# Depthwise convolution taps of the sample tokens: from VectorE to GpSimd, one tap of all four chunks with each step of the page loads

## Chip, cores and metric

The kernel runs on one core of a Trainium2 chip. The metric is the time of one execution on the device in microseconds (us), here the median of three runs. TensorE's clock has two levels, 1.2 and 2.4 GHz; the profile gives the granted clock as a share of the full one.

## What is computed

One layer of a decoder with two groups of tokens, 1024 of a prompt and 64 of samples (8 sequences of 8 new tokens). Every token passes three branches (a convolution module, sparse attention over selected keys, attention over a memory), which are merged and followed by a feed-forward part. Two pieces matter here. They don't depend on each other.

```python
# convolution: 31 taps per channel (512 channels), for prompt and sample tokens
c = conv(u_ext, w_dw)                 # c[t, ch] = sum_k u_ext[t + k, ch] * w_dw[k, ch]
c = silu(layernorm(c + b_dw, g_ln, b_ln))
# indexer scores of the sample tokens over 4096 cached keys each, which lie in pages of 128
ki_past = cache_idx_k[page_table]
I = sum_h w[t, h] * relu(q_idx[t, h] . ki[s] / 8)
```

For the sample tokens `u_ext` is 30 cached rows and 8 new ones of each sequence.

## The kernel before, in words

The program is a row of stages. Each is a block with a program of its own for every engine; at its end all engines meet at a barrier (`end_phase`, L2619 to L2624), and semaphores are cleared. `build` (L2610) calls the stages in order; the one that matters is `stage_sample_score` (L2018), between the first and the second half of the input products.

In this stage two things go on side by side.

The first is the scoring of the cached keys, in 32 steps (`NSTEP`). A step takes 8 pages, four for each of two sequences. Four of them go into one half of a slot and four into the other; there are four slots (`NSL`). The loads are shared out: SP issues three pages of the first sequence, GpSimd three of the second, ScalarE the fourth of both (`load_page`, L2035). A load reads the page's number into a register (L2039) and issues a DMA (L2040). From step 4 on, the issuing engine first waits until TensorE has turned the pages of four steps ago (`s_turn`). TensorE transposes the four pairs of pages of a step (`turn`, L2061, products on L2067), ScalarE copies the result out of PSUM (L2122), TensorE forms the dot products (`dots`, L2075), ScalarE applies relu (L2128), and TensorE adds up the heads (`wsum`, L2083). At the end come four small pairs of products for the new keys (L2098, L2101) with a relu between them (L2138).

The second is the convolution, on VectorE (L2141 to L2161). Channels lie on the partitions in four chunks (`KC`), tokens along the free dimension. For each of 31 taps (`CW`) and each chunk there are two instructions, one for the 1024 prompt tokens and one for the 64 sample tokens, each of which multiplies by the tap's weight of the channel and adds to what stands in `cT`. Tap 0 starts from the bias instead (L2152), the others are fused (L2155). A tap of a chunk waits for the tap before of the same chunk, four pairs earlier (L2147). When all taps are done, VectorE waits for the last weighted sum of TensorE and adds a mask to it (L2159), which is the last operation of the stage.

The order of the work on an engine is the order in which the program is written; nothing reorders it. GpSimd has nothing in this stage but its 96 loads:

```python
            def load_pages(eng, par):
                for n in range(NSTEP):
                    if n >= NSL:
                        eng.wait_ge(s_turn, n - NSL + 1)
                    for g in range(PPC - 1):
                        load_page(eng, page_in[par], n, g, par)
```

The prediction also reads rows of other stages, for what GpSimd and VectorE take there: the sample part of the gated input on GpSimd (L1153), the last scaling of the layer norm on VectorE (L1657), the split of the merge weights on GpSimd (L2281) beside a sum on VectorE (L2252), the split of the merged activations on both (L2322), a scaled difference on VectorE (L2495), and the indirect loads of keys by GpSimd (L689).

Of the kernel before, what the change touches and what calls it, by code (L numbers as in the profile page):

```python
# [11 lines left out]
F32 = mybir.dt.float32  # L12
# [3 lines left out]
ALU = mybir.AluOpType  # L16
# [3 lines left out]
P = 128  # L20
# [3 lines left out]
SEQ = 1024  # L24
NSEQ, TDEC = 8, 8
NS = NSEQ * TDEC
NT = SEQ + NS
# [4 lines left out]
DC, CW = 512, 31  # L32
KC = DC // P
# [37 lines left out]
PPC = 4  # L71
# [1946 lines left out]
def stage_sample_score(nc, m, score):  # L2018

    NQ = 2 * NPAIR  # L2020
    NSTEP = NC2 * NQ
    with ExitStack() as ctx:
        NSL = 4
# [4 lines left out]
        page_in = [[m.sem(f"ik_page_in_{e}{i}") for i in range(NSL)] for e in ("sync", "gpsimd", "scalar")]  # L2028

        s_turn, s_kev = m.sem("ik_page_turned"), m.sem("ik_T_ready")  # L2030
        s_dots, s_relu, s_ws = m.sem("ik_dots"), m.sem("ik_relu_s"), m.sem("ik_wsum")
        s_hev = [m.sem(f"ik_half_evac{i}") for i in range(2)]
        s_end, tap = m.sem("ik_end"), m.sem("conv_taps")
        with nc.Block() as block:
            def load_page(eng, arrived, n, g, par):  # L2035
                r, q = n // NQ, n % NQ
                hf, i = q // NPAIR, q % NPAIR
                at = r * PPC + (2 * i + par) * NPAGE + hf * NC2 * PPC + g
                phys = eng.value_load(m.pages[0:1, at:at + 1], min_val=0, max_val=NPHYS - 1)  # L2039
                eng.dma_start(page[:, n % NSL, g, par, :].rearrange("p (a d) -> p a d", a=1),  # L2040
                              m.cache_idx_k[bass.ds(phys, 1)].rearrange("a p d -> p a d")).then_inc(arrived[n % NSL], 16)

            def load_pages(eng, par):

                for n in range(NSTEP):
                    if n >= NSL:
                        eng.wait_ge(s_turn, n - NSL + 1)
                    for g in range(PPC - 1):
                        load_page(eng, page_in[par], n, g, par)

            @block.sync
            def _(sp):
                load_pages(sp, 0)

            @block.gpsimd
            def _(pool):
                load_pages(pool, 1)

            @block.tensor
            def _(pe):  # L2060
# [80 lines left out]
            @block.vector  # L2141
            def _(dve):
                nc.vector.memset(score[0:64, HALF:SW], NEG).then_inc(s_end, 1)
                for k in range(CW):
                    for c in range(KC):
                        if k >= 1:
                            dve.wait_ge(tap, 2 * ((k - 1) * KC + c + 1))  # L2147
                        for dst, src in ((m.cT[:, c, 0:SEQ], m.u[:, c, k:k + SEQ]),
                                         (m.cT[:, c, SEQ:NT].rearrange("p (s t) -> p s t", s=NSEQ),
                                          m.us[:, c, :, k:k + TDEC])):  # L2150
                            if k == 0:
                                nc.vector.tensor_scalar(dst, src, m.wdw[:, c, 0:1], m.bdw_sb[:, c:c + 1],  # L2152
                                                        ALU.mult, ALU.add).then_inc(tap, 1)
                            else:
                                nc.vector.scalar_tensor_tensor(out=dst, in0=src, scalar=m.wdw[:, c, k:k + 1], in1=dst,  # L2155
                                                               op0=ALU.mult, op1=ALU.add).then_inc(tap, 1)
                dve.wait_ge(tap, 2 * CW * KC)
                dve.wait_ge(s_ws, NSTEP + NPAIR)
                nc.vector.tensor_tensor(score[64:128, HALF:SW], m.B[5][64:128, 0:NS], m.newmask[64:128, :], ALU.add  # L2159
                                        ).then_inc(s_end, 1)  # L2160
                dve.wait_ge(s_end, 2)  # L2161
# [448 lines left out]
def build(nc, io):  # L2610
    with ExitStack() as ctx:
# [62 lines left out]
        stage_first_products(nc, m)  # L2674
        end_phase()
        stage_sample_score(nc, m, m.sscore)
        end_phase()
        c_ki.close()
# [75 lines left out]
```

## Time and profile before

| | |
|---|---|
| median of 3 runs | 2603.65 us (2603.33 to 2607.54) |
| profiled execution: its time, its span | 2609.0 us, 2607.4 us |
| busy over the span | TensorE 86%, VectorE 51%, GpSimd 31%, ScalarE 23% |
| mean granted TensorE clock | 0.928 |
| the stage | from 540.6 us, closing add at 711.6 us, next stage from 713.2 us |

Times in the rows are us from the start of the span unless marked ns. PE is TensorE, PEld its weight loads, DVE VectorE, ACT ScalarE, POOL GpSimd. A timeline row has the start, the duration, the engine, the line, the operation, what it writes and reads, the shape and the count, and in brackets the idle time before it with what ended it. A group of instructions has busy time and mean ns of one, and then the idle time before them. Neighbouring instructions of an engine overlap by some hundredths of a us, so what one costs is the distance of starts. "issue" is time in which an engine waited for nothing that the profile shows.

### The profile page before, as it was taken

The numbers are of one execution on the slowest core, as the hardware profiler recorded it, in microseconds if no ns is written. First come the engines' busy times: TensorE is split into PE (matmuls) and PEld (weight loads), VectorE is DVE, ScalarE is ACT, GpSimd is POOL, SyncE is SP. The second block draws the span as 40 slices with busy tenths as digits, with TensorE's granted clock in tenths as the row PEclk, the third lists the DMA queues.
The fourth block names the chain that finished last, engine by engine and source line by source line (L and its number), as shares of the span: only waits on it lengthen the run. The fifth ranks groups of instructions, "written<-read, shape, count | busy, mean of one in ns | idle before, by whom it ended". The sixth has DMA issues, their size and how long they took to land. (4 is left out here: it accounts for less than half of the span.)

```text
span 2607.4 us, 37427 instructions
## 1 busy us (share of the span) xinstructions
PE 2229.6 (86%) x14085; PEld 2044.7 (78%) x14102; DVE 1338.9 (51%) x2216; ACT 596.2 (23%) x1066; POOL 801.2 (31%) x591
## 2 busy tenths in 40 slices
PE   5959988967289998666667879699999999999997
PEld 5829988932079998555445679698999999999997
DVE  5089998079959992395677454433111111111123
ACT  4152212223031211132233331222210111111112
POOL 4102211134011221257667412434222231222231
PEclk9988998989599999886688999899999999999999
DMA  5001112223032221467877434411111111111112
GB/s 178 21 17 50 47 45 89 84 72 75 1 126 90 92 66 41 163 212 265 279 222 229 136 129 139 157 48 40 41 40 53 44 36 53 41 46 43 49 32 93
DMA packets 229221, 240.04 MB, mean 92 GB/s; under 512 B 37011, under 2 KB 192704, under 8 KB 226669
## 3 DMA queue, kind: packets, MB, share of 16 engines
q1 hardware_dynamic: 183723, 124.76, 16.2%
q0 software_dynamic: 23552, 70.28, 8.6%
q10 hardware_dynamic: 21834, 43.55, 4.5%
q8 instruction: 66, 1.08, 0.2%
q14 instruction: 46, 0.38, 0.0%
HBM read 207.91 MB, written 30.98 MB: 92 GB/s over the span
## 5 line engine op out<-in xcount | busy, mean ns | idle before, releaser
L387 PE MATMUL banks<-ffn_in_hi,ffn_w_hi 128*128 128x384 f32 (+1 forms) x1032 | 339.1, 329 | 5.3 <-POOL ffn_w_lo L402 3.8
L388 PE MATMUL banks<-ffn_in_lo,ffn_w_hi 128*128 128x384 f32 (+1 forms) x1032 | 338.8, 328 | 0.0
L389 PE MATMUL banks<-ffn_in_hi,ffn_w_lo 128*128 128x384 f32 (+1 forms) x1032 | 338.8, 328 | 0.0
L402 POOL TENSOR_TENSOR ffn_w_lo<-ffn_w_raw,ffn_w_hi 128x1024 fp32r<-128x1024 f32 (+2 forms) x84 | 180.4, 2148 | 409.1 <-ACT ffn_w_hi L201 409.1
L387 PE MATMUL banks<-halves,ffn_w_hi 128*128 128x384 f32 (+1 forms) x654 | 214.4, 328 | 22.7 <-PEq L2324 22.7
L389 PE MATMUL banks<-halves,ffn_w_lo 128*128 128x384 f32 (+1 forms) x654 | 214.3, 328 | 0.0
L388 PE MATMUL banks<-halves,ffn_w_hi 128*128 128x384 f32 (+1 forms) x654 | 214.2, 328 | 0.0
L387 PEld LDWEIGHTS banks<-ffn_in_hi,ffn_w_hi 128*128 128x128 f32 x1032 | 195.1, 189 | 6.1 <-issue 4.0
L387 PE MATMUL banks<-h_hi,second_w_hi 128*128 128x384 f32 (+1 forms) x576 | 190.6, 331 | 7.3 <-POOL second_w_lo L235 5.6
L388 PEld LDWEIGHTS banks<-ffn_in_lo,ffn_w_hi 128*128 128x128 f32 x1032 | 195.0, 189 | 0.0
L389 PEld LDWEIGHTS banks<-ffn_in_hi,ffn_w_lo 128*128 128x128 f32 x1032 | 195.0, 189 | 0.0
L389 PE MATMUL banks<-h_hi,second_w_lo 128*128 128x384 f32 (+1 forms) x576 | 189.9, 330 | 0.0
L388 PE MATMUL banks<-h_lo,second_w_hi 128*128 128x384 f32 (+1 forms) x576 | 189.9, 330 | 0.0
L689 POOL DMA_INDIRECT k_rows_got<-in_cache_k,sel_row x128 | 137.6, 1075 | 144.3 <-POOLq L2623 62.4
L2155 DVE SCALAR_TENSOR_TENSOR room<-room,w_dw 128x1024 f32<-128x1024 f32 x240 | 167.1, 778 | 0.0
L1305 DVE TENSOR_SCALAR_CACHE_REDUCE mask<-room,sel_cand 128x384 bf16<-128x384 f32 (+1 forms) x186 | 163.7, 942 | 1.1
L387 PE MATMUL banks<-h_hi,first_w_hi 128*128 128x384 f32 (+1 forms) x480 | 160.2, 334 | 4.3 <-POOL first_w_lo L402 4.3
L388 PE MATMUL banks<-h_lo,first_w_hi 128*128 128x384 f32 (+1 forms) x480 | 159.7, 333 | 0.0
L389 PE MATMUL banks<-h_hi,first_w_lo 128*128 128x384 f32 (+1 forms) x480 | 159.7, 333 | 0.0
L2295 DVE TENSOR_TENSOR x<-banks,x 128x384 f32 (+1 forms) x96 | 50.9, 536 | 205.4 <-PE banks L389 183.3
L699 POOL DMA_INDIRECT v_rows_got<-in_cache_v,sel_row x128 | 129.3, 1010 | 67.5 <-issue 37.5
L201 ACT CAST ffn_w_hi<-ffn_w_raw 128x1024 fp32r<-128x1024 f32 (+2 forms) x84 | 79.2, 944 | 307.4 <-PE banks L389 281.2
(377 smaller groups left out, 4847.5 us busy)
## 6 DMA issues: line engine op xcount, KB each, us to landing
ffn_w_raw<-in_w_ffn_in SPq DMA_DIRECT2D x44, 512.0 KB, 3.7
merge_gate<-gate_spill_dram SPq DMA_DIRECT2D x24, 544.0 KB, 3.9
first_w_raw<-in_w_in SPq DMA_DIRECT2D x24, 512.0 KB, 3.8
second_w_raw<-in_w_in SPq DMA_DIRECT2D x24, 512.0 KB, 3.8
ffn_w_raw<-in_w_ffn_out SPq DMA_DIRECT2D x24, 384.0 KB, 3.3
gate_spill_dram<-second_out ACTq DMA_DIRECT2D x16, 544.0 KB, 2.7
room<-q_spill_dram ACTq DMA_DIRECT2D x8, 1024.0 KB, 6.9
q_spread<-q_spill_dram ACTq DMA_DIRECT2D x8, 1024.0 KB, 6.6
```

The lines of the kernel that those rows point to most:

```text
L201: self.m.nc.scalar.copy(self.w_hi[:, s, 0:g.kc, :], self.raw[:, s, 0:g.kc, :]).then_inc(self.hi_done, 1)
L387: nc.tensor.matmul(out, self.w_hi[:, s, k, :], g.hi[:, k, a:a + w], start=(k == 0), stop=False)
L388: nc.tensor.matmul(out, self.w_hi[:, s, k, :], g.lo[:, k, a:a + w], start=False, stop=False)
L389: mm = nc.tensor.matmul(out, self.w_lo[:, s, k, :], g.hi[:, k, a:a + w], start=False, stop=(k == g.kc - 1))
L402: self.m.nc.gpsimd.tensor_tensor(self.w_lo[:, s, 0:g.kc, :], self.raw[:, s, 0:g.kc, :], self.w_hi[:, s, 0:g.kc, :], ALU.subtract).then_inc ...
L689: pool.indirect_dma_start(self.keys[:, n % self.K_SLOTS, f, :], None, rows, bass.IndirectOffsetOnAxis(ap=m.sel_row[:, f, n:n + 1], axis=0) ...
L699: pool.indirect_dma_start(self.values[:, v % self.V_SLOTS, f, :], None, rows, bass.IndirectOffsetOnAxis(ap=m.sel_row[:, f, v:v + 1], axis= ...
L1305: c = nc.vector.tensor_scalar(m.mask[:, MOFF[b]:MOFF[b + 1]], sl(b), lim, 0.0, op, ALU.add, accum_out=cnt[:, j:j + 1])
L2155: nc.vector.scalar_tensor_tensor(out=dst, in0=src, scalar=m.wdw[:, c, k:k + 1], in1=dst, op0=ALU.mult, op1=ALU.add).then_inc(tap, 1)
L2295: nc.vector.tensor_tensor(x, m.B[3 * s + n][:, 0:w].rearrange("p (a n) -> p a n", a=1), x, ALU.add).then_inc(gemm.emptied[s], 1)
```

## The change

VectorE keeps the prompt part of each tap only. GpSimd takes the sample part: after the three loads of step n (n below 31) it does tap n for all four chunks at once, as a product of 4 x 8 x 8 columns with a broadcast weight into a new buffer, and an add of that product to `cT` (for tap 0: of the product to the broadcast bias). The add waits for the product, the product for the add of the tap before. VectorE's counts of its own semaphore are halved, and at the end it waits for all 62 operations of GpSimd as well. SP's loads stay as they are.

```diff
-                for n in range(NSTEP):
-                    if n >= NSL:
-                        eng.wait_ge(s_turn, n - NSL + 1)
-                    for g in range(PPC - 1):
-                        load_page(eng, page_in[par], n, g, par)
+            def load_pages_of(eng, par, n):
+                if n >= NSL:
+                    eng.wait_ge(s_turn, n - NSL + 1)
+                for g in range(PPC - 1):
+                    load_page(eng, page_in[par], n, g, par)
...
             def _(pool):
-                load_pages(pool, 1)
+                made = ctx.enter_context(nc.sbuf_tensor("conv_sample_product", [P, KC, NS], F32))
+                made4 = made[:, :, :].rearrange("p c (s t) -> p c s t", s=NSEQ)
+                out = m.cT[:, :, SEQ:NT].rearrange("p c (s t) -> p c s t", s=NSEQ)
+
+                def sample_tap(k):
+                    w = m.wdw[:, :, k].unsqueeze(2).unsqueeze(3).to_broadcast([P, KC, NSEQ, TDEC])
+                    if k >= 1:
+                        pool.wait_ge(stap, 2 * k)
+                    nc.gpsimd.tensor_tensor(made4, m.us[:, :, :, k:k + TDEC], w, ALU.mult).then_inc(stap, 1)
+                    pool.wait_ge(stap, 2 * k + 1)
+                    b = m.bdw_sb[:, :].unsqueeze(2).unsqueeze(3).to_broadcast([P, KC, NSEQ, TDEC])
+                    nc.gpsimd.tensor_tensor(out, made4, out if k else b, ALU.add).then_inc(stap, 1)
+
+                for n in range(NSTEP):
+                    load_pages_of(pool, 1, n)
+                    if n < CW:
+                        sample_tap(n)
...
                         if k >= 1:
-                            dve.wait_ge(tap, 2 * ((k - 1) * KC + c + 1))
-                        for dst, src in ((m.cT[:, c, 0:SEQ], m.u[:, c, k:k + SEQ]),
-                                         (m.cT[:, c, SEQ:NT].rearrange("p (s t) -> p s t", s=NSEQ),
-                                          m.us[:, c, :, k:k + TDEC])):
...
+                            dve.wait_ge(tap, (k - 1) * KC + c + 1)
+                        dst, src = m.cT[:, c, 0:SEQ], m.u[:, c, k:k + SEQ]
...
-                dve.wait_ge(tap, 2 * CW * KC)
+                dve.wait_ge(tap, CW * KC)
+                dve.wait_ge(stap, 2 * CW)
                 dve.wait_ge(s_ws, NSTEP + NPAIR)
```

## Rows read from the trace of the kernel before

**Rows 1.** Timeline of VectorE, in short windows of the stage.

```profile
540.64 3.92 DVE L2152 TENSOR_SCALAR room<-room,w_dw,params 128x1024 f32<-128x1024 f32 x8
544.48 1.27 DVE L2155 SCALAR_TENSOR_TENSOR room<-room,w_dw 128x1024 f32<-128x1024 f32 x1
...
545.67 0.27 DVE L2155 SCALAR_TENSOR_TENSOR room<-room,w_dw 128x64 f32<-128x64 f32 x1
...
545.87 1.27 DVE L2155 SCALAR_TENSOR_TENSOR room<-room,w_dw 128x1024 f32<-128x1024 f32 x1
...
547.07 0.27 DVE L2155 SCALAR_TENSOR_TENSOR room<-room,w_dw 128x64 f32<-128x64 f32 x1
...
711.60 0.23 DVE L2159 TENSOR_TENSOR room<-banks,newmask 64x64 f32<-64x64 f32 x1
```

**Rows 2.** Groups of instructions, shapes apart, from 530 to 760 us.

```profile
L2155 DVE SCALAR_TENSOR_TENSOR room<-room,w_dw 128x1024 f32<-128x1024 f32 x120 | 153.4, 1278 | 0.0
L2155 DVE SCALAR_TENSOR_TENSOR room<-room,w_dw 128x64 f32<-128x64 f32 x120 | 33.4, 278 | 0.0
...
L1657 DVE SCALAR_TENSOR_TENSOR room<-room,params,second_out 128x1088 f32<-128x1088 f32 x1 | 1.4, 1350 | 1.2 <-ACT second_out L1594 1.2
...
L2040 POOL DMA_DIRECT2D ik_page<-in_cache_idx_k x96 | 51.6, 537 | 85.0 <-issue 79.6 <-PE banks L2067 5.5
```

**Rows 3.** Stretches: length; busy PE, PEld, DVE, ACT, POOL; PE clock, DMA, GB/s.

```profile
600.00:653.00 53.00, 38.17 (x123) 13.40 (x122) 53.00 (x78) 20.06 (x35) 24.46 (x46) 1.00 0.31 74
653.00:665.00 12.00, 8.68 (x31) 3.69 (x30) 12.00 (x18) 3.63 (x9) 0.12 (x1) 0.96 0.01 3
665.00:711.00 46.00, 0.00 (x0) 0.00 (x0) 46.00 (x67) 0.00 (x0) 0.00 (x0) 0.50 0.00 0
724.00:729.00 5.00, 0.00 (x0) 0.00 (x0) 4.96 (x12) 2.10 (x3) 2.38 (x2) 0.98 0.59 148
729.00:733.00 4.00, 3.98 (x14) 3.98 (x15) 0.00 (x0) 2.10 (x2) 2.31 (x1) 0.59 0.60 148
```

**Rows 4.** Timeline of GpSimd: third and fourth page load, and the last.

```profile
544.42 0.53 POOL L2040 DMA_DIRECT2D ik_page<-in_cache_idx_k  x1 [0.57 <-issue]
545.57 0.53 POOL L2040 DMA_DIRECT2D ik_page<-in_cache_idx_k  x1 [0.62 <-issue]
...
652.59 0.53 POOL L2040 DMA_DIRECT2D ik_page<-in_cache_idx_k  x1 [0.61 <-issue]
```

**Rows 5.** Timeline of TensorE: its last products of the stage.

```profile
664.41 0.48 PE L2101 MATMUL banks<-ik_relu,w_sel 128*64 128x64 f32 x2 [0.31 <-ACT ik_relu L2138]
```

**Rows 6.** Lines L1153 and L2281: duration min/median/max in ns, first and last start.

```profile
L1153 POOL TENSOR_TENSOR u_new<-glu_pair x4: 320/322/325, 237.4 to 309.4; 128x64 f32<-128x64 f32 x4
...
L2281 POOL TENSOR_TENSOR merge_w_lo<-merge_w_raw,merge_w_hi x24: 1262/1569/2210, 1520.5 to 1660.5; 128x512 fp32r<-128x512 f32 x24
```

**Rows 7.** Timelines of GpSimd and VectorE where the merged activations are split.

```profile
1674.40 2.48 POOL L2322 TENSOR_TENSOR halves<-room,halves 128x1088 fp32r<-128x1088 f32 x1 [12.64 <-ACT halves L2336]
...
1676.84 3.53 POOL L2322 TENSOR_TENSOR halves<-room,halves 128x1088 fp32r<-128x1088 f32 x1
...
1675.36 2.68 DVE L2322 TENSOR_TENSOR halves<-room,halves 128x1088 fp32r<-128x1088 f32 x1 [2.56 <-ACT halves L2336]
...
1677.96 3.57 DVE L2322 TENSOR_TENSOR halves<-room,halves 128x1088 fp32r<-128x1088 f32 x1
...
1681.45 3.57 DVE L2322 TENSOR_TENSOR halves<-room,halves 128x1088 fp32r<-128x1088 f32 x1
```

**Rows 8.** Timelines of GpSimd and VectorE in the merge.

```profile
1558.87 2.21 POOL L2281 TENSOR_TENSOR merge_w_lo<-merge_w_raw,merge_w_hi 128x512 fp32r<-128x512 f32 x1 [4.66 <-ACT merge_w_hi L2261]
...
1558.65 1.29 DVE L2252 TENSOR_TENSOR room<-room,merge_gate 128x1088 f32<-128x1088 f32 x1
```

**Rows 9.** Line L2495: duration min/median/max in ns, first and last start.

```profile
L2495 DVE SCALAR_TENSOR_TENSOR ffn_in_lo<-x,params,ffn_in_hi x8: 2425/2428/2429, 1710.2 to 1793.2; 128x1088 fp32r<-128x1088 f32 x8
```

**Rows 10.** Timeline of GpSimd: an indirect load right behind another.

```profile
1082.64 0.96 POOL L689 DMA_INDIRECT k_rows_got<-in_cache_k,sel_row  x1 [0.30 <-issue]
```

More of the change, by code:

```diff
@@ L2032, in stage_sample_score @@
         s_hev = [m.sem(f"ik_half_evac{i}") for i in range(2)]
-        s_end, tap = m.sem("ik_end"), m.sem("conv_taps")
+        s_end, tap, stap = m.sem("ik_end"), m.sem("conv_taps"), m.sem("conv_sample_taps")
         with nc.Block() as block:
@@ L2041, in load_page @@
                               m.cache_idx_k[bass.ds(phys, 1)].rearrange("a p d -> p a d")).then_inc(arrived[n % NSL], 16)
-            def load_pages(eng, par):
-                for n in range(NSTEP):
-                    if n >= NSL:
-                        eng.wait_ge(s_turn, n - NSL + 1)
-                    for g in range(PPC - 1):
-                        load_page(eng, page_in[par], n, g, par)
+            def load_pages_of(eng, par, n):
[3 more added lines that the diff above has]
+                    load_page(eng, page_in[par], n, g, par)
             @block.sync
             def _(sp):
-                load_pages(sp, 0)
+                for n in range(NSTEP):
+                    load_pages_of(sp, 0, n)
             @block.gpsimd
             def _(pool):
-                load_pages(pool, 1)
+                made = ctx.enter_context(nc.sbuf_tensor("conv_sample_product", [P, KC, NS], F32))
[9 more added lines that the diff above has]
+                    nc.gpsimd.tensor_tensor(out, made4, out if k else b, ALU.add).then_inc(stap, 1)
+                for n in range(NSTEP):
+                    load_pages_of(pool, 1, n)
+                    if n < CW:
+                        sample_tap(n)
             @block.tensor
@@ L2146, in _ @@
                         if k >= 1:
-                            dve.wait_ge(tap, 2 * ((k - 1) * KC + c + 1))
-                        for dst, src in ((m.cT[:, c, 0:SEQ], m.u[:, c, k:k + SEQ]),
-                                         (m.cT[:, c, SEQ:NT].rearrange("p (s t) -> p s t", s=NSEQ),
-                                          m.us[:, c, :, k:k + TDEC])):
[L2151 to L2156, printed above, removed]
-                dve.wait_ge(tap, 2 * CW * KC)
+                            dve.wait_ge(tap, (k - 1) * KC + c + 1)
+                        dst, src = m.cT[:, c, 0:SEQ], m.u[:, c, k:k + SEQ]
+                        if k == 0:
+                            nc.vector.tensor_scalar(dst, src, m.wdw[:, c, 0:1], m.bdw_sb[:, c:c + 1],
+                                                    ALU.mult, ALU.add).then_inc(tap, 1)
+                        else:
+                            nc.vector.scalar_tensor_tensor(out=dst, in0=src, scalar=m.wdw[:, c, k:k + 1], in1=dst,
+                                                           op0=ALU.mult, op1=ALU.add).then_inc(tap, 1)
+                dve.wait_ge(tap, CW * KC)
+                dve.wait_ge(stap, 2 * CW)
                 dve.wait_ge(s_ws, NSTEP + NPAIR)
```

## Prediction

> **What bounds the kernel now.** I read the stage that the diff touches and nothing else, because a barrier stands before it and behind it: whatever its end moves by, the run moves by. The first view is the timeline of VectorE. The convolution starts at 540.64 us and runs without a gap until the closing add (L2159) at 711.60 [rows 1]. The groups by shape say of what: 120 taps of 128x1024 and 120 of 128x64 [rows 2]. The reader is to see the starts, not the durations, since neighbours overlap: the small tap at 545.67 is followed by a large one at 545.87 and by the next small one at 547.07 [rows 1]. So a small tap holds VectorE for 0.20 us (its duration says 0.27) and a large one for 1.20, which makes 1.39 for a pair, and 120 such pairs from 544.48 on (167 us) are the rest of the stretch.
>
> The second view is busy time by stretch. TensorE and ScalarE are done by 665: from 665 to 711 VectorE alone works, TensorE at 1.2 GHz (granted 0.50) doing nothing [rows 3]. So the pages have 46 us of slack, and the question is how much of it the change eats.
>
> The third is the timeline of GpSimd. It issues 96 page loads, three to a step, one start every 1.14 to 1.15 us (544.42, 545.57), each 0.53 of work on the engine and 0.61 of issue, the last at 652.59 [rows 2, 4]. TensorE ends 12.3 us after that last issue, at 664.41 + 0.48 = 664.89 [rows 5]. GpSimd's program order therefore paces the pages at 3 x 1.145 = 3.43 us a step, and what is put between its loads delays the pages directly. Its waits on turned pages come to 5.5 us in all [rows 2].
>
> **The change part by part.**
>
> *Removed from VectorE:* 4 + 120 small taps. 124 x 0.196 = 24.3 us (0.20 unrounded). Alone, the convolution would end at 711.6 - 24.3 = 687.3. The four taps k = 0 lose four small ones too, so the first fused tap starts at 543.7 instead of 544.48. The halved semaphore counts cost nothing: a tap still waits for the one four instructions earlier.
>
> *Added to GpSimd:* 31 products and 31 adds of 128x256. The same operation took 0.322 us for 64 columns and, undisturbed, 1.262 for 512 [rows 6]: 2.10 ns a column, so 0.725 us for 256. The broadcast weight and the 4x8x8 patterns are not in the trace; I take no surcharge, with 0 and +0.3 us as bounds. 62 x 0.725 = 45 us of bare work, by itself inside the slack of 46.
>
> *Both engines at once.* This decides. Where VectorE and GpSimd run operations with two SBUF inputs side by side, they take turns [rows 7]: GpSimd's first operation, begun before VectorE's, took 2.48 us, its next one 3.53, and VectorE's went to 2.68 and 3.57, while an operation of that size alone takes VectorE 1.29 [rows 8]. In the steady part both have a pitch of 3.49 (1677.96 to 1681.45), which is one VectorE turn (about 1.21) plus one GpSimd turn (2.28). [rows 8] show the same from one side: the VectorE operation ends at 1559.94, GpSimd's 512 columns at 1561.08, 1.14 later, against 1.262 alone. So a GpSimd turn is its duration less 0.12 to 0.20: 0.53 to 0.60 for 256 columns, and I take 0.58. VectorE's operation ends 1.16 after GpSimd's (1680.37 to 1681.53 in [rows 7]); for 1024 columns instead of 1088, 1.08. The convolution's own instruction is of this kind: the fused form with two SBUF inputs took 2.43 us at all eight places where GpSimd was subtracting beside it [rows 9], and 1.35 elsewhere [rows 2].
>
> The opposite reading deserves its price. The Trainium skill, "Advanced Engine Details and Errata", section VectorE Performance Modes, warns of blocking between GpSimd and Vector instructions in a two-port mode, and names no others. The fused tap is in no faster mode (1.20 us for 1024 columns, 1.17 ns each), so by that note alone nothing would be blocked and the time would be that of the first rival, 2597; by the turns of [rows 7] it is 2627. The trace disagrees with the note as far as it goes, since [rows 7, 9] slow down all the same.
>
> *VectorE with turns:* 687.3 + 62 x 0.58 = 723.3. That is already 12 us behind today's end.
>
> *GpSimd with turns.* Let an add end at time 0. VectorE's waiting tap ends at 1.08, the next at 2.28, the next at 3.47. GpSimd issues three loads, starts 1.145 apart, the third finished 2.82 after the first starts; the first starts 0 to 0.6 after the add. (The row nearest is the gap between back-to-back indirect issues, 0.30 [rows 10], and I take that; 0.6 is the idle time before a page load [rows 4].) The product thus asks at 2.8 to 3.4, before 3.47, and gets its turn there: over at 4.05. The add waits for the product by semaphore, so VectorE gets the turn between (5.13), and the add ends at 5.71. So a tap and its step take **5.71 us** instead of 3.43, and VectorE does four taps in it, which is the one k that those four chunks make: both queues finish nearly together.
>
> The first product asks at 544.95, when the third load is done [rows 4]. VectorE's tap just then ends at 544.95 too, so I count the next (546.15); the other choice is worth 1.2 us. The add of k = 0 then ends at 548.4, that of k = 30 at 548.4 + 30 x 5.71 = 719.7. Behind it on GpSimd's queue stand the loads of step 31: the last starts at 719.7 + 0.3 + 2.29 = 722.3, and 12.3 us of tail follow, as today. The closing add starts at 734.6 instead of 711.6: **+23.0 us**.
>
> *The new waits.* VectorE's wait for all sample taps is over at 719.7, long before its wait for the last weighted sum: nothing. The product's wait for the former add is over too. The add's wait for the product is in the sum (it gives VectorE its turn between). What queues behind on GpSimd is the three loads of the next step, for which TensorE waits, then ScalarE's copies and its own two loads (behind the copies in its queue), then VectorE at the very end. The loads on SP go further ahead and wait for turned pages: nothing.
>
> *TensorE's clock.* In today's page loop it stands at 2.4 GHz with 38.2 us busy in 53 [rows 3]. The same work would spread over 5.71 us a step. From 724 to 729 TensorE did nothing, and the products after it ran at a granted 0.59 [rows 3]. Should the level fall in the page loop too, the tail with its 8.7 busy us [rows 3] would grow, by 0 to about 6 us; I take 0, the level that the page loop has today, and keep the 6. After the stage, the memory's second products start behind a weight transfer issued after the barrier, which shifts with it: 0, with up to 1.5 us to win if the clock is higher there.
>
> The profiled execution took 2609.0 us (span 2607.4), the median is 2603.65. Both stages are the same work, so I put the +23 on the median: 2626.65, **2627**.
>
> **The rivals.**
>
> *No turns for these shapes* (not slower). VectorE ends at 687.3; The add, once sent off, runs under the preparation of the next load, so a step is three loads of 1.145, the 0.53 of the third that the product must wait for, 0.73 of product and some 0.07 of hand-over: 4.76. The add of k = 30 would end near 689.5, the last load start at 692, the stage end at 704.3, which is -7 us: 2597, and -3 if the add is not covered. It decides once a tap costs the page loop less than 46.7 / 31 = 1.5 us. The idle 0.61 before each load is for it; [rows 7, 9] are against it.
>
> *VectorE alone sets the end.* If GpSimd prepares loads while its add waits, the product could ask before 2.28; the step is then 4.52, the pages end near 699, and VectorE's 723.3 decides: +12, 2616. For it: preparation and work of two loads do overlap. Against: the loads' own 2.82.
>
> *A turn later.* If a load can start only 0.65 us or more after the add, or the product costs 0.3 more, the request misses the boundary at 3.47 and the step is 6.91 with five VectorE taps. After 24 such taps VectorE is done, the last six go at some 4.9: add k = 30 at 745, end at 760: +48, 2652.
>
> **How the numbers follow.** Forecast (2622 to 2634 with the clock's bound): 0.63. VectorE's end alone: 0.13. A turn later: 0.14. No turns: 0.08. Something past 2652: 0.02. The range takes in the two slower rivals and leaves out the last two: 2613 to 2652. A measurement of this kernel tells 0.2% (5.2 us) from no change. No turns lies on both sides of that, so faster 0.05, same 0.04, slower 0.91.
>
> **What would show it.** In the changed profile: large taps 1.20 apart where GpSimd loads, and about 1.78 (1.20 + 0.58) apart around a product or an add; products and adds of 0.7 us drawn out to 1.2 to 1.9; triples of page loads about 5.7 us apart instead of 3.43; the last load near 722; the closing add near 735, released by TensorE and no longer by VectorE's own taps. Taps 1.20 apart all the way would prove me wrong about the turns, a last load before 705 about what sets the end, and steps of 6.9 about the boundary.

## The result, and the profile after

The changed kernel takes 2614.96 us (median of seven executions, the lowest 2609.41) against 2603.65 before. The ratio is 1.0036 with an interval of 1.0023 to 1.0049, so it is 9.4 us (6.0 to 12.8) slower. One of the seven executions, and four of six in a later comparison, took 2738 to 2741 us; the ratios are of the others, and the second half of the experiments is about the long ones. The profiled execution took 2618.74 us, its span is 2617.1.

The difference lies in the one stage. The timeline of VectorE in the changed kernel, in short windows: the stage's first instruction, four neighbouring prompt taps, the closing add:

```profile
540.80 0.11 DVE L2158 MEMSET room<- 64x64 f32 x1 [93.28 <-PEq L2637]
...
568.22 1.27 DVE L2168 SCALAR_TENSOR_TENSOR room<-room,w_dw 128x1024 f32<-128x1024 f32 x1
...
569.41 1.92 DVE L2168 SCALAR_TENSOR_TENSOR room<-room,w_dw 128x1024 f32<-128x1024 f32 x1
...
571.25 1.74 DVE L2168 SCALAR_TENSOR_TENSOR room<-room,w_dw 128x1024 f32<-128x1024 f32 x1
...
572.92 1.27 DVE L2168 SCALAR_TENSOR_TENSOR room<-room,w_dw 128x1024 f32<-128x1024 f32 x1
...
721.88 0.23 DVE L2173 TENSOR_TENSOR room<-banks,newmask 64x64 f32<-64x64 f32 x1
```

From first instruction to closing add are 181.1 us, against 171.0 before [rows 1]; what follows takes 1895.2 after and 1895.8 before. Read the starts: an undisturbed tap still costs 1.20 (568.22 to 569.41), the next two 1.84 and 1.67. The small taps are gone, and the closing add has no idle time before it: VectorE's own taps still set the end.

GpSimd in the same stretch, one step of the pages, and its last load:

```profile
567.16 0.57 POOL L2040 DMA_DIRECT2D ik_page<-in_cache_idx_k  x1
567.90 0.53 POOL L2040 DMA_DIRECT2D ik_page<-in_cache_idx_k  x1 [0.17 <-issue]
569.04 0.53 POOL L2040 DMA_DIRECT2D ik_page<-in_cache_idx_k  x1 [0.61 <-issue]
569.60 0.64 POOL L2064 TENSOR_TENSOR conv_sample_product<-room,w_dw 128x256 f32<-128x256 f32 x1
570.32 1.60 POOL L2067 TENSOR_TENSOR room<-conv_sample_product,room 128x256 f32<-128x256 f32 x1
571.86 0.57 POOL L2040 DMA_DIRECT2D ik_page<-in_cache_idx_k  x1
...
692.69 0.53 POOL L2040 DMA_DIRECT2D ik_page<-in_cache_idx_k  x1 [0.61 <-issue]
```

A step is 571.86 - 567.16 = 4.70 us (3.43 before, [rows 4]; 5.71 predicted). Two things are to be seen. The first load of the next step starts at 571.86, when the add ends: it was prepared while the add still waited. And the product (569.60) takes 0.64 us, its bare time, although VectorE had begun a tap at 569.41; it is that tap that grows to 1.92. Only the add waits (1.60). So a step holds three taps of VectorE and what the two operations hold them up by: 3 x 1.20 + 0.64 + 0.47 = 4.71.

Two of the 31 products of this profile did wait, and theirs are the only steps above 5.1 us. One of them:

```profile
552.13 0.57 POOL L2040 DMA_DIRECT2D ik_page<-in_cache_idx_k  x1
552.88 0.53 POOL L2040 DMA_DIRECT2D ik_page<-in_cache_idx_k  x1 [0.17 <-issue]
554.34 0.53 POOL L2040 DMA_DIRECT2D ik_page<-in_cache_idx_k  x1 [0.93 <-issue]
554.89 1.25 POOL L2064 TENSOR_TENSOR conv_sample_product<-room,w_dw 128x256 f32<-128x256 f32 x1
556.22 1.58 POOL L2067 TENSOR_TENSOR room<-conv_sample_product,room 128x256 f32<-128x256 f32 x1
557.75 0.58 POOL L2040 DMA_DIRECT2D ik_page<-in_cache_idx_k  x1
```

Its third load came 0.32 us later than in other steps, the product asked 0.50 us into a tap, waited (1.25), and the step took 557.75 - 552.13 = 5.62 us with a fourth tap in it. The other late one asked at 0.48 us and took 1.29; the 29 that asked 0.17 to 0.47 us into a tap all took 0.63 to 0.65.

The groups of instructions of the changed kernel, shapes apart, from 530 to 780 us, answer to [rows 2]:

```profile
L2168 DVE SCALAR_TENSOR_TENSOR room<-room,w_dw 128x1024 f32<-128x1024 f32 x120 | 178.1, 1561 | 0.0
...
L2040 POOL DMA_DIRECT2D ik_page<-in_cache_idx_k x96 | 53.0, 552 | 51.8 <-issue 51.8
L2067 POOL TENSOR_TENSOR room<-conv_sample_product,room 128x256 f32<-128x256 f32 x30 | 48.0, 1599 | 2.4
L2064 POOL TENSOR_TENSOR conv_sample_product<-room,w_dw 128x256 f32<-128x256 f32 x31 | 21.0, 678 | 0.5
```

And the stretches (columns as in [rows 3]), with TensorE's last products of the stage from its timeline behind them:

```profile
600.00:653.00 53.00, 36.32 (x93) 12.06 (x94) 53.00 (x35) 14.06 (x24) 43.15 (x57) 0.81 0.24 57
...
705.00:721.00 16.00, 0.08 (x1) 0.00 (x0) 16.00 (x15) 0.00 (x0) 0.00 (x0) 0.50 0.00 0
```

```profile
704.61 0.47 PE L2116 MATMUL banks<-ik_relu,w_sel 128*64 128x64 f32 x2 [0.31 <-ACT ik_relu L2153]
```

The pages are done at 705.08, and 16 of the 46 us of slack are left. TensorE's granted clock in the page loop went from 1.00 to 0.81, but its tail from the last load on is 12.4 us against 12.3 before [rows 4, 5]; in the tail the granted clock was 0.92, against 0.96 before [rows 3].

### The profile page after: what moved, and what is told of

Read it like the earlier page. It is cut to its first block and busy times, and to the rows that moved or that the text cites. A ratio compares the mean times of both kernels' runs of the same rounds, so it can differ in the third digit from the quotient of the medians.

```text
span 2617.1 us, 37382 instructions
## 1 busy us (share of the span) xinstructions
PE 2256.7 (86%) x14102; PEld 2054.1 (78%) x14102; DVE 1348.3 (52%) x2092; ACT 596.2 (23%) x1066; POOL 867.2 (33%) x653
## 5 line engine op out<-in xcount | busy, mean ns | idle before, releaser
L2168 DVE SCALAR_TENSOR_TENSOR room<-room,w_dw 128x1024 f32<-128x1024 f32 x120 | 178.1, 1561 | 0.0
```

## The experiments

All stage lengths are from the stage's first instruction on VectorE to its closing add: 171.0 us in the kernel before, 181.1 in the changed one.

**No sample taps.** Both engines leave them out.

```diff
                 for n in range(NSTEP):
                     load_pages_of(pool, 1, n)
-                    if n < CW:
-                        sample_tap(n)
...
-                dve.wait_ge(stap, 2 * CW)
```

> Leaves out the sample tokens' taps on both engines. Turns (each of GpSimd's 62 operations holds VectorE up by 0.56 us, and VectorE sets the end): large taps 1.196 apart all the way, closing add near 687.5, about 24 us below the kernel before and 34 below the changed one; the page loop ends near 665 as before. Rival (VectorE is slowed by something else that stays, such as the page loads of GpSimd): the taps stay drawn out and the closing add stays above 700.

Ratio to the kernel before 0.9896 (0.9880 to 0.9913); stage 146.5 us. The taps' group:

```profile
L2166 DVE SCALAR_TENSOR_TENSOR room<-room,w_dw 128x1024 f32<-128x1024 f32 x120 | 143.6, 1273 | 0.0
```

143.6 us is what 120 prompt taps take alone. So the small taps cost VectorE 171.0 - 146.5 = 24.5 us before, and GpSimd's 62 operations now hold it up by 178.1 - 143.6 = 34.5, 0.56 each. The difference is the 10 us.

**GpSimd only writes.**

```diff
-                    nc.gpsimd.tensor_tensor(made4, m.us[:, :, :, k:k + TDEC], w, ALU.mult).then_inc(stap, 1)
+                    nc.gpsimd.memset(made[:, :, :], 0.0).then_inc(stap, 1)
...
-                    nc.gpsimd.tensor_tensor(out, made4, out if k else b, ALU.add).then_inc(stap, 1)
+                    nc.gpsimd.memset(made[:, :, :], 0.0).then_inc(stap, 1)
```

> Each product and each add on GpSimd is replaced by a memset of the same 128x256 into the product's buffer, with the same waits: GpSimd writes but reads nothing of SBUF; the sample taps are left out. Turns over reading (VectorE's second input and GpSimd's inputs come by one way): taps 1.196 apart, closing add near 687.5, page loop's last load below 690. Rival (any operation of GpSimd takes VectorE's turn): each memset costs VectorE 0.2 to 0.5 us, closing add at 700 to 718.

Ratio 0.9925 (0.9907 to 0.9943). Groups from 530 to 900 us:

```profile
L2168 DVE SCALAR_TENSOR_TENSOR room<-room,w_dw 128x1024 f32<-128x1024 f32 x120 | 143.6, 1280 | 0.0
L2173 DVE TENSOR_TENSOR room<-banks,newmask 64x64 f32<-64x64 f32 x1 | 0.2, 227 | 8.3 <-PE banks L2116 8.3
...
L2064 POOL MEMSET conv_sample_product<- 128x256 f32 x31 | 10.2, 331 | 0.0
```

The taps are undisturbed, 143.6 us, so it is GpSimd's reading that collides. The expected closing add was missed: it waits 8.3 us for the pages, which even with memsets of 0.33 us take 4.37 a step.

**One SBUF input on GpSimd** (a single execution, so the groups are read and not the time).

```diff
-                    nc.gpsimd.tensor_tensor(made4, m.us[:, :, :, k:k + TDEC], w, ALU.mult).then_inc(stap, 1)
+                    nc.gpsimd.tensor_copy(made4, m.us[:, :, :, k:k + TDEC]).then_inc(stap, 1)
...
-                    nc.gpsimd.tensor_tensor(out, made4, out if k else b, ALU.add).then_inc(stap, 1)
+                    nc.gpsimd.tensor_copy(out, made4).then_inc(stap, 1)
```

> Product and add on GpSimd are replaced by copies of the same 128x256 (one SBUF input each); the sample taps' arithmetic is left out. Theory (what counts is that GpSimd reads SBUF while VectorE has two SBUF inputs): copies hold VectorE up too, by less, 0.1 to 0.4 us each, 6 to 25 us over all taps. Rival (only operations with two inputs on both sides take turns): taps 1.196 apart throughout, as with the memsets, and the pages set the end near 693.

```profile
L2168 DVE SCALAR_TENSOR_TENSOR room<-room,w_dw 128x1024 f32<-128x1024 f32 x120 | 152.6, 1347 | 0.0
...
L2067 POOL COPY room<-conv_sample_product 128x256 f32<-128x256 f32 x31 | 38.7, 1249 | 1.9
L2064 POOL COPY conv_sample_product<-room 128x256 f32<-128x256 f32 x31 | 30.8, 994 | 0.0
```

The groups show 152.6 - 143.6 = 9.0 us, 0.15 per copy: reading one operand is enough. The execution took 2609.11 us, since the pages now set the end: the closing add, at 713.71, waits 20.0 us for them. The Trainium skill, "SBUF — State Buffer", section Who interferes with whom, states the rule: a Vector instruction with two SBUF inputs collides with a GpSimd instruction that reads SBUF, not with one that only writes. The groups agree: 120 taps take 178.1 us beside products and adds, 152.6 beside copies, 143.6 beside memsets. The section of the Trainium skill that the prediction weighed, "Advanced Engine Details and Errata", VectorE Performance Modes, names two-port modes alone and leaves this case out.

**Half of the taps moved.** GpSimd does taps 0 to 14, VectorE 15 to 30 after a wait for GpSimd's last.

```diff
-                    if n < CW:
+                    if n < 15:
                         sample_tap(n)
...
+                        if k >= 15:
+                            late = m.cT[:, c, SEQ:NT].rearrange("p (s t) -> p s t", s=NSEQ)
+                            nc.vector.scalar_tensor_tensor(out=late, in0=m.us[:, c, :, k:k + TDEC],
+                                                           scalar=m.wdw[:, c, k:k + 1], in1=late,
+                                                           op0=ALU.mult, op1=ALU.add).then_inc(tap, 1)
```

> Taps 0 to 14 of the sample tokens on GpSimd as in the changed kernel, taps 15 to 30 on VectorE as in the kernel before. Theory (each tap moved saves VectorE 4 x 0.196 = 0.785 us and costs it 1.115 in turns, VectorE sets the end either way): from the stage's start to the closing add 171.0 + 15 x 0.33 = 176.0 us, against 171.0 before and 181.1 with all moved. Rival (there is a best split between the two engines): below 171.

Stage 175.3 us, ratio 1.0023 (1.0011 to 1.0035); all ten executions took 2606.03 to 2611.31 us. The loss goes with the number of taps moved (4.3 us for 15, 10.1 for 31), and this split, the only one that was run, gains nothing.

**The loads wait for the add.** This undoes the overlap seen in the step above.

```diff
                     nc.gpsimd.tensor_tensor(out, made4, out if k else b, ALU.add).then_inc(stap, 1)
+                    pool.wait_ge(stap, 2 * k + 2)
```

> GpSimd waits for its add before it prepares the next step's loads. Theory (the prediction's step of 5.71 us failed because the loads' preparation runs under the waiting add, so that the product asks 2.4 us after the add and not 2.8 to 3.4): the product now asks some 4.0 us after the add, past the boundary at 3.5, gets its turn at 4.7, and the step is about 6.8 us; VectorE is done near 714, the page loop ends near 759, closing add there: 47 us above the kernel before. Rival (preparation plays no part, the loads wait for the add anyway): the step stays at 4.7 and the closing add at 722.

Ratio 1.0185 (1.0165 to 1.0205), stage 218.1 us. GpSimd's timeline, one step, and then VectorE's closing add:

```profile
611.50 0.53 POOL L2040 DMA_DIRECT2D ik_page<-in_cache_idx_k  x1 [0.57 <-issue]
612.64 0.54 POOL L2040 DMA_DIRECT2D ik_page<-in_cache_idx_k  x1 [0.60 <-issue]
613.19 1.09 POOL L2064 TENSOR_TENSOR conv_sample_product<-room,w_dw 128x256 f32<-128x256 f32 x1
614.36 1.59 POOL L2067 TENSOR_TENSOR room<-conv_sample_product,room 128x256 f32<-128x256 f32 x1
617.17 0.58 POOL L2040 DMA_DIRECT2D ik_page<-in_cache_idx_k  x1 [1.22 <-issue]
...
620.00 1.10 POOL L2064 TENSOR_TENSOR conv_sample_product<-room,w_dw 128x256 f32<-128x256 f32 x1
```

```profile
759.25 0.23 DVE L2174 TENSOR_TENSOR room<-banks,newmask 64x64 f32<-64x64 f32 x1 [51.16 <-PE banks L2117]
```

The step is 6.81 us (613.19 to 620.00), the closing add at 759.25 and released by TensorE, as the theory had it; VectorE ends 51.16 us earlier, at 708.1 (near 714 was expected). The product asks 0.66 us into a tap and waits here (1.09), and a step holds five taps. So the preparation under the waiting add is what lets the product ask early in a tap in the changed kernel.

**Sample taps on ScalarE and TensorE.**

```diff
+                    if n < CW:
+                        pe.wait_ge(s_made, KC * (n + 1))
+                        nc.tensor.matmul(m.B[6][:, 0:KC * NS], m.ident[:, :],
+                                         made[:, n % NSL].rearrange("p c t -> p (c t)"),
+                                         start=(n == 0), stop=(n == CW - 1)).then_inc(s_added, 1)
...
+                    if n < CW:
+                        if n >= NSL:
+                            act.wait_ge(s_added, n - NSL + 1)
+                        for c in range(KC):
+                            nc.scalar.activation(made[:, n % NSL, c, :].rearrange("p (s t) -> p s t", s=NSEQ),
+                                                 m.us[:, c, :, n:n + TDEC], ACT.Identity, scale=m.wdw[:, c, n:n + 1]
+                                                 ).then_inc(s_made, 1)
...
+                act.wait_ge(s_added, CW)
+                for c in range(KC):
+                    nc.scalar.activation(m.cT[:, c, SEQ:NT], m.B[6][:, c * NS:(c + 1) * NS], ACT.Identity,
+                                         bias=m.bdw_sb[:, c:c + 1]).then_inc(stap, 1)
```

> The sample taps go to engines that take no turns with VectorE: ScalarE forms the four products of a tap (128x64, scaled by the weight) with each step's loads, TensorE adds them up in PSUM with one product by the identity per step, ScalarE adds the bias at the end. Turns: VectorE's taps are 1.196 apart and end near 687.5; the page loop takes up to 1 us a step more (665 to 697), so the closing add lies at 688 to 698, 14 to 24 us below the kernel before. Rival (the move costs VectorE time wherever it goes, or ScalarE's four extra operations slow the page loop past VectorE): closing add above 711.

Ratio 0.9918 (0.9901 to 0.9934): it beats both kernels, by some 21 us the one before. The stage takes 146.5 us, as with no sample taps at all. ScalarE's group from 538 to 690 us, and TensorE's last products:

```profile
L2128 ACT ACTIVATE conv_sample_product<-room,w_dw 128x64 f32<-128x64 f32 x124 | 33.5, 341 | 41.6 <-PE banks L2098 28.1 <-issue 12.0 <-PE banks L2069 1.5
```

```profile
663.63 0.47 PE L2108 MATMUL banks<-ik_relu,w_sel 128*64 128x64 f32 x2 [0.31 <-ACT ik_relu L2156]
```

33.5 us of products lie in ScalarE's gaps: the pages end 125.4 us after the stage's first instruction (664.10 - 538.66), against 124.3 before, far ahead of VectorE.

**Two memsets ahead of each product,** meant to make the product ask later in a tap.

```diff
+                    nc.gpsimd.memset(idle[:, 0], 0.0)
+                    nc.gpsimd.memset(idle[:, 1], 0.0)
                     nc.gpsimd.tensor_tensor(made4, m.us[:, :, :, k:k + TDEC], w, ALU.mult).then_inc(stap, 1)
```

> The changed kernel with two memsets of 128x256 (0.3 us each, nothing read) on GpSimd before each product, so that the product asks some 0.6 us later in VectorE's tap. Theory (a product that asks within the first 0.47 us of a tap's recorded time goes before it, a later one waits for the tap's end, as the prediction had it for all): the product asks 0.78 us into the tap, takes 1.0 instead of 0.63, the step is 5.6 us instead of 4.7, the last load lies near 720 and the closing add near 732, set by the pages; VectorE's tap is held up 0.36 by the product instead of 0.70, so that its taps end earlier than in the changed kernel, near 714. Rival (0.6 us more of work a step, no boundary): step 5.3, last load 711, closing add 723.

Neither came: 2754.55 us, ratio 1.0581 (1.0557 to 1.0606). GpSimd's timeline:

```profile
547.34 142.10 POOL L2067 TENSOR_TENSOR conv_sample_product<-room,w_dw 128x256 f32<-128x256 f32 x1
```

One product takes 142 us. It ends half a us after VectorE's last prompt tap (688.96), and VectorE's taps are undisturbed throughout. GpSimd was passed over by 118 of the 120 taps, and its loads, and so the pages, stood behind that product; after it the page loop runs its 31 remaining steps alone. So turns aren't granted as a matter of course.

**Where in the tap?** The first theory was that the place in VectorE's tap at which the product asks decides. One extra instruction ahead of the convolution shifts VectorE by 0.72 us and touches nothing on GpSimd, two shift it by 1.45, and one memset instead of two shifts the product by 0.3.

```diff
                 nc.vector.memset(score[0:64, HALF:SW], NEG).then_inc(s_end, 1)
+                nc.vector.tensor_scalar(again[:, 0, :], m.u[:, 0, 0:SEQ], m.wdw[:, 0, 0:1], m.bdw_sb[:, 0:1], ALU.mult, ALU.add)
```

> The changed kernel with one more instruction like a k = 0 tap on VectorE (0.72 us, into a scratch buffer) ahead of the convolution: nothing on GpSimd is touched, only the first product now asks some 0.75 us into a tap of VectorE instead of 0.28. Theory (where in a tap the product asks decides, and around 0.77 it is passed over for good, as the 142 us product of the run with two memsets was): the first product takes some 142 us, the closing add comes near 845 to 860, 2740 to 2755 us in all, as in the one execution of 2740.65. Rival (the memset right ahead of the product did it): as the changed kernel and 0.7 us more, 2612 to 2620.

> Two such instructions instead of one (1.45 us), so that the first product asks at the very start of a tap. Theory (the place in the tap decides): the changed kernel's rhythm of 4.7 us a step is back, closing add near 723.5. Rival (any shift of VectorE locks GpSimd out): 2740 or more.

> The changed kernel with one memset of 0.3 us ahead of each product instead of two: the first product asks about 0.55 us into the tap. Theory (the place decides; at 0.48 to 0.66 a product waited for the tap's end and then had its turn): no lock-out; the product waits up to 0.75 us, steps of 5.3 to 5.7, closing add at 720 to 733. Rival (a memset ahead of the product locks it out): closing add near 850 as with two.

> The changed kernel as it is, in more executions. Theory (it stays clear of the lock-out only by where its first product falls in a tap, which hardly moves from run to run): most executions at 2609 to 2619 us, an occasional one near 2740; none in between. Rival (2740 was a disturbance of its own): none near 2740 in these, or some at other times.

All three came out locked, at 2741.11, 2741.89 and 2749.65 us. The theory fell: the products asked 0.75, 0.23 and 0.52 us into a tap. The memset isn't needed for it, by the first two, but "any shift of VectorE" isn't either, since the unshifted kernel did it in four of these six executions (median 2738.24) and in the other two took 2611.87 and 2613.52. GpSimd in the profiled one:

```profile
543.44 142.60 POOL L2064 TENSOR_TENSOR conv_sample_product<-room,w_dw 128x256 f32<-128x256 f32 x1
```

Its product asked 0.27 us into the tap that begins at 543.17, that of the first profile 0.28 us and that of the run with the waiting loads, which got in too, 0.26: the place doesn't tell them apart. The rate does differ between comparisons. The half-moved kernel and the one with the waiting loads are the changed kernel up to the first product, and none of their 10 and 4 executions was locked; the four of six came in one series of executions on one chip, in which the shifted kernels and the one with a single memset ran too. So the three locked runs don't show that the shift or the memset did it. What raised the rate there is open; the chip alone isn't needed, since two memsets (4 of 4) and the taps begun a step later (below, 4 of 4) locked on two others.

**How to get GpSimd in.** Three kernels: the shifted one (one extra instruction, locked in both executions) with a wait of VectorE for GpSimd's tap before last; the changed one with a wait of VectorE for the first product alone; the changed one with GpSimd's taps begun a step later.

```diff
                 for k in range(CW):
+                    if k >= 2:
+                        dve.wait_ge(stap, 2 * (k - 1))
```

> The run with the one extra instruction ahead of the convolution, in which the first product was passed over in every execution, and a wait on VectorE: tap k of the prompt starts when GpSimd's tap k-2 is done. Theory (a product is passed over only as long as VectorE's taps follow each other without a gap): VectorE stops at k = 2 after some 9 us at most, the product gets its turn there, and the rest goes on in turns: first product at most 9 us, closing add at 725 to 740, all executions within 2612 to 2635. Rival (GpSimd is held up by something that lasts 142 us in itself): closing add above 840, or GpSimd is passed over again and again, above 760.

```diff
                 for k in range(CW):
+                    if k == 1:
+                        dve.wait_ge(stap, 1)
```

> The changed kernel with a wait on VectorE between tap 0 and tap 1 of the prompt until GpSimd's first product is done (some 2 us of VectorE). Theory (it is the first product, which meets VectorE's undisturbed row of taps, that is passed over; once the engines have taken one turn they go on so): no execution near 2740, all at 2610 to 2622, closing add near 724. Rival (any product or add can be passed over): some executions well above 2640.

```diff
-                    if n < CW:
-                        sample_tap(n)
+                    if n >= 1:
+                        sample_tap(n - 1)
```

> GpSimd's taps start one step of the pages later, when VectorE is in its fifth undisturbed fused tap instead of its second. Theory (an operation that meets an undisturbed row can be passed over wherever in the row): some or all executions near 2740. Rival (only the first two or three fused taps are dangerous): none, all at 2610 to 2622.

With the guard all five executions took 2609.72 to 2621.29 us (ratio 1.0042, 1.0025 to 1.0059). GpSimd's timeline, and VectorE's around the wait:

```profile
542.24 4.60 POOL L2065 TENSOR_TENSOR conv_sample_product<-room,w_dw 128x256 f32<-128x256 f32 x1
546.92 0.61 POOL L2068 TENSOR_TENSOR room<-conv_sample_product,params 128x256 f32<-128x256 f32 x1
```

```profile
545.09 1.28 DVE L2172 SCALAR_TENSOR_TENSOR room<-room,w_dw 128x1024 f32<-128x1024 f32 x1
...
547.57 1.28 DVE L2172 SCALAR_TENSOR_TENSOR room<-room,w_dw 128x1024 f32<-128x1024 f32 x1 [1.20 <-POOL room L2068]
```

The product is passed over by four taps, VectorE runs into its wait at 546.37, and the product is done 0.48 us later. After a second wait of VectorE (0.61 us, at 553.44) the engines take turns as in the changed kernel (4.70 a step; closing add at 720.09, before the 725 to 740 expected; stage 182.2). In the six locked profiles, too, the product ends 0.48 us after VectorE's last tap. So a lock ends when VectorE's row has a gap. With the first product let in ahead of the row, all five executions took 2613.37 to 2621.18 (ratio 1.0047, 1.0033 to 1.0062); as the changed kernel got in without that in eight of 13, five are few, and that this suffices rests as much on no later operation having locked in any profile. A step later, all four took 2733.58 to 2736.69, with a product of 139 us: a row met in its fifth tap locks as well. In all six locked profiles it is the first product, and after a first turn no product or add took longer than about 1.6 us. Why a first product that finds the row running sometimes gets in (eight of 13 executions of the changed kernel) is open.

## Why the prediction was right and wrong

*Sign, place and cause* were right: slower, by VectorE and GpSimd reading SBUF in turns, all of it in this stage (in the executions that took turns). Removing both sides of the exchange gives its two terms: 24.5 us saved (24.3 in the sum), 34.5 paid (62 x 0.58 = 36.0). VectorE's end was put at 723.3 and came at 721.84.

*The size was wrong, 9 to 11 us instead of 23*, by the step "GpSimd with turns": 5.71 us for a tap and its page step, which measured 4.70. Two of its terms failed, and it took both. "The first starts 0 to 0.6 after the add": it started 0.05 before the add's recorded end, and the second only 0.74 later instead of 1.145. So the product asked 2.4 us after the add, not 2.8 to 3.4. That alone would have changed nothing, for 2.4 still lies between the prediction's boundaries at 2.28 and 3.47, where the sum has the product wait. The other term is the rule for the turn, "asks before 3.47, and gets its turn there": the product asked 0.18 us into the tap that began at 2.2 and went first, so a step holds three taps and not four; a request at 2.8 to 3.4 would have come 0.6 us or more into that tap, where none went first. Where a product of the same profile asked later, at 0.50, it did wait as predicted, and the step took 5.62, close to the 5.71 of the sum. That the loads' preparation ran under the waiting add is shown by making them wait: the step moved to 6.81 and the end to 759. (The row chosen as nearest for it, an indirect load behind another, has no waiting operation to hide under.) Why an early request goes ahead of a tap that has begun is open.

The rival "VectorE alone sets the end" (12 us, 2616) is what happened, and its cause, preparation while the add waits, was there. But the request came after its 2.28, and it held because of the early turn, which no part of the prediction has: that was in part luck.

*The turns' price* was nearly right in sum and wrong in its parts. A product that goes first costs its tap 0.64 us (1.84 - 1.20), an add that waits 0.47 (1.67 - 1.20); a product that waits costs 0.36 (with the waiting loads, the tap behind one starts the next 1.56 later instead of 1.20). So VectorE's end, 721.84 for 723.3, was hit with two parts that err in opposite ways: 0.64 and 0.47 for 0.58 and 0.58.

*The rival "no turns"* is refuted by the tap starts. *The clock's bound*, 0 to 6 us, came to 0.1: the granted clock fell to 0.81 in the page loop, but stood at 0.92 in the tail.

*What no part foresaw:* that turns can fail. The prediction took alternation from two stages where it held and made it a rule; there the row was at most four operations long, here it is 120. In the locked executions the change costs some 135 us, far above the range.

## To carry to other kernels

Work moved to GpSimd isn't off VectorE while VectorE has a row of operations with two SBUF inputs: price it at what it holds VectorE up by (here 1.11 us per tap for 0.79 saved), and look first at ScalarE and TensorE, which hid the same work completely. Where both must read SBUF, give the row a semaphore wait that bounds how far VectorE can run ahead, or let GpSimd's first operation go before the row (five executions speak for that), above all if anything else (here the page loads) stands behind it on GpSimd's queue. And repeat such a kernel often: eight executions of 13 looked like a loss of 0.4%, the other five were 5% slower.

## What the runs showed of the hardware that was not expected

- GpSimd's first 128x256 product waited 139 to 144 us while VectorE ran 115 to 119 fused taps back to back, in six profiles; it was done within half a us of VectorE's row ending or pausing. The Trainium skill, "SBUF — State Buffer", section Who interferes with whom, says of VectorE's two-port modes that whoever issues first gets the port pair shared with GpSimd for the whole instruction while the other is blocked. These runs, with fused operations of two SBUF inputs, show that GpSimd need not get in between back-to-back instructions of VectorE at all.
- Once the engines had taken turns, the place of the request in VectorE's tap decided: in five profiles (the changed kernel, half the taps, the waiting loads, and the two with a wait of VectorE), products that asked up to 0.47 us into a tap's recorded time went first, those that asked at 0.48 to 0.98 waited for its end.
- In a step of the turns, GpSimd prepared its next load while its add still waited for VectorE; the load started within 0.05 us of the add's end.
- A GpSimd copy with one SBUF input held VectorE up by 0.15 us, a memset of the same size by nothing, a product or an add by 0.36 to 0.64 each.
